# Four-quadrant 64x64 products in the delta stage of a diffusion trunk: two of four heads cross the partition halves

## The chip, the core and the metric

The kernel runs on one core of one Trainium2 chip. The metric is the device time of one execution in microseconds (us). Three runs of the kernel before gave 3064.36 us as median, from 3062.11 to 3075.93.

## The reference

Two layers of a transformer trunk over 512 latent and 256 context tokens of width 1024. Each layer projects its normalised input, feeds three token mixers (grouped-query attention, neighbourhood attention, and a bidirectional gated delta rule), merges their outputs, and ends with a squared-ReLU MLP. The change touches the delta rule alone. It works on chunks of 64 tokens, for 4 heads and in two directions. For each chunk and head it inverts a 64x64 triangular matrix by repeated squaring:

```
nil = where(strict, -einsum('bhid,bhjd->bhij', kb, kc) * decay, 0)
tinv = eye(CHUNK) + nil
power = nil
for _ in range(int(math.log2(CHUNK)) - 1):      # five times
    power = power @ power
    tinv = tinv + tinv @ power
w_v = tinv @ (vc * beta)
k_cd = tinv @ (kb * exp(gc))
```

The chunks' results then go through a recurrence over a 128x128 state per head.

## The kernel before, in words

Five engines run their own instruction streams and meet at semaphores. Nothing reorders them: the order of the work is the order in which the program is written for each engine. PE is the matrix engine (a weight load, PEld, goes with each matmul), DVE, ACT and POOL are the element-wise engines, SP issues the DMAs of the weights.

**Stages.** A layer runs: normalisation, the delta rule's projections and short convolution, the delta stage (this case), the attention projections, attention, gates and branches, output, MLP. Large products are done in three passes of split halves (L453 to L455).

**The delta stage.** A layer has 6 steps `s`. A step treats one tile of 128 tokens for each direction `d` (0 and 1), so the two partition halves (rows 0 to 63 and 64 to 127) hold two chunks, and 4 heads lie side by side: 8 matrices of 64x64 for each `d`. A step has a *powers phase* and a *recurrence*.

In the powers phase, iteration `i` (0 to 4) squares the power and its transpose and multiplies the inverse:
- PE, `halves` (L609): for each head and each half, one 64x64 product whose operands lie in one partition half and whose result lands in the same half. The array thus uses two of its four 64x64 quadrants. For each `d`: 8 products for the power, and 8 for its transpose (not in the last iteration), into one PSUM pair ("pw"); then, once these are read out, 8 products power x inverse into another ("X"). In the trace every float32 product leaves two records.
- ACT (L1266) copies the new power out of PSUM, DVE (L1686) the new transpose; DVE (L1690) adds the product to the inverse.
- In layer 0, in 20 of the 30 iterations (3 or 4 in each step, none in `i` = 4), PE also does a block of the later layers' modulation from weights that SP streams in (L490, `modulation`, 32 products of 32 columns on four column strips, 4 slots of 512 KB through a ring of 6), and later one transpose (L500).

PSUM is a ring of four pairs (`take`): each product group takes the next and waits until the group four before it was read. Before the powers phase, PE turns the matrix (L609 `ps<-cst,R`, "AT"), ACT copies it (L1252), DVE adds the identity (L1669). After it, PE computes k_cd (L798), then the recurrence: L817, L825, L837, L848, L859, with the next step's L633 (key products), read out by DVE (L1710, L1719 or L1721, L1649, L1658) and ACT (L1280). In layer 1 only the last four steps have outputs (L837, L859, L1719, L1721).

Of the kernel before, what the change touches and what calls it, by code (L numbers as in the profile page):

```python
# [21 lines left out]
P = 128  # L22
# [86 lines left out]
def program(nc, a, out, x_store, skew, bias_rows, z_store, book):  # L109
    book["final"] = book.get("final", False)  # L110
    with ExitStack() as ctx:
# [138 lines left out]
        def power(d, i):  # L250

            one, two = (pbuf[d], tbuf[d]), (p2buf[d], t2buf[d])
            return (*one, *two) if i % 2 == 0 else (*two, *one)

# [185 lines left out]
        def _(pe):  # L440
# [171 lines left out]

            def head_spread(l, j):
# [67 lines left out]
            for l in range(DEPTH):  # L681
# [83 lines left out]
                for s in range(TT):  # L765
                    turned = None
                    for i in range(5):
                        for d in range(2):
                            src, srcT, dst, dstT = power(d, i)
                            pe.wait_ge(*(read("pw", l, s, d, i - 1) if i else read("AT", l, s)))  # L770
                            ps = take(pe, "pw", l, s, d, i)
                            last = halves(ps, srcT, src)
                            if i < 4:
                                last = halves(ps[:, 512:768], src, srcT)
                            last.then_inc(*filled("pw", l, s, d, i))
                        for d in range(2):
# [14 lines left out]
                    for d in range(2):  # L791
                        pe.wait_ge(*pool_done.at("kbe", l, s, d))
                        pe.wait_ge(*read("X", l, s, d, 4))
# [259 lines left out]
        def _(act):  # L1053
# [88 lines left out]
            for l in range(DEPTH):  # L1142
# [105 lines left out]
                def delta_turned(l, s):  # L1248

                    act.wait_ge(*full("AT", l, s))  # L1250
                    for d in range(2):
                        A(flat(tbuf[d]), pair("AT", l, s)[:, 512 * d:512 * d + 256], ACT.Copy)\  # L1252
                            .then_inc(*free("AT", l, s, by=1))
# [157 lines left out]
        def _(dve):  # L1411
# [128 lines left out]
            for l in range(DEPTH):  # L1540
# [101 lines left out]
                def delta_decays(l, s, d):  # L1642

                    dve.wait_ge(*full("bc", l, s, d))
                    if s:
                        dve.wait_ge(*(pool_done.at("QW", l, s - 1, d) if want_out(l, tiles[0][s - 1]) else dve_done.at("A", l, s - 1, d)))
# [17 lines left out]
                def delta_turned(l, s, d):  # L1664
# [472 lines left out]
```

## Time and profile before

| | |
|---|---|
| median of 3 runs | 3064.36 us |
| span of the profiled execution | 3063.6 us |
| its own time beyond the span | not recorded; the median is 0.8 us above the span |
| PE busy | 2885.9 us (94%) |
| PEld busy | 2477.4 us (81%) |
| DVE, ACT, POOL busy | 1198.7, 1040.4, 1039.7 us (39, 34, 34%) |

A page has the busy times of each engine, the span in 40 slices, the DMA queues, the chain of work that ended last, and groups of instructions by line with their count, busy time and mean duration, and what ended the engine's idle time before them. The starts of instructions are read from a timeline. A matmul's duration holds its way through the array, so a busy PE may still be starting instructions more slowly than it could.

### The profile page before, as it was taken

How to read it: one execution, taken by the hardware profiler on the slowest of the kernel's cores; microseconds unless marked ns; L12 is line 12 of the kernel's file. 1: busy time of each engine (PE TensorE's matmuls, PEld its weight loads, DVE VectorE, ACT ScalarE, POOL GpSimd, SP SyncE). 2: the span in 40 equal slices, each digit the busy share in tenths (PEclk: the TensorE clock that was granted, in tenths of full speed). 3: DMA queues.
4: the chain of work that ended last, by engine and by line, in shares of the span. 5: the costliest groups of instructions: out<-in, count | busy, mean ns of one | idle time of the engine just before them, and what ended most of it. 6: DMA issues, size and time to landing. Idle time of an engine off the chain costs nothing. (4 is left out here: it accounts for less than half of the span.)

```text
span 3063.6 us, 57689 instructions
## 1 busy us (share of the span) xinstructions
PE 2885.9 (94%) x24931; PEld 2477.4 (81%) x24931; DVE 1198.7 (39%) x1821; ACT 1040.4 (34%) x1771; POOL 1039.7 (34%) x701
## 2 busy tenths in 40 slices
PE   6999888998899999999999999898999999999999
PEld 5877777886688888799999978788787788778887
DVE  4753443245631113422222268555245721242223
ACT  4542222225542112422222245433225532342223
POOL 3234434230313333222232322355330344434443
PEclk8999999999999999999999999999999999999999
DMA  6225434110012232122222122100220034323332
GB/s 251 62 87 197 141 138 125 49 49 1 12 36 62 62 106 67 49 65 67 62 69 62 62 90 62 37 3 10 83 56 8 13 98 139 93 82 97 96 99 81
DMA packets 303693, 231.96 MB, mean 76 GB/s; under 512 B 16785, under 2 KB 275281, under 8 KB 302545
## 3 DMA queue, kind: packets, MB, share of 16 engines
q1 hardware_dynamic: 296816, 203.53, 22.0%
q0 software_dynamic: 3776, 17.91, 1.6%
q10 hardware_dynamic: 2848, 6.82, 0.6%
q8 instruction: 199, 3.26, 0.4%
q14 instruction: 54, 0.43, 0.0%
HBM read 217.22 MB, written 11.98 MB: 75 GB/s over the span
## 5 line engine op out<-in xcount | busy, mean ns | idle before, releaser
L1892 POOL TENSOR_TENSOR wl<-wring,wh 128x1024 fp32r<-128x1024 f32 (+1 forms) x312 | 725.9, 2328 | 1342.3 <-ACT wh L1124 1335.8
L453 PE MATMUL ps<-hh,wh 128*128 128x496 f32 (+2 forms) x2344 | 832.2, 355 | 6.5 <-DVE R L1743 3.5
L455 PE MATMUL ps<-hh,wl 128*128 128x496 f32 (+2 forms) x2344 | 820.3, 350 | 0.0
L454 PE MATMUL ps<-hl,wh 128*128 128x496 f32 (+2 forms) x2344 | 820.2, 350 | 0.0
L453 PEld LDWEIGHTS ps<-hh,wh 128*128 128x128 f32 x2344 | 441.7, 188 | 69.6 <-issue 6.6
L454 PEld LDWEIGHTS ps<-hl,wh 128*128 128x128 f32 x2344 | 442.1, 189 | 57.1 <-issue 3.8
L455 PEld LDWEIGHTS ps<-hh,wl 128*128 128x128 f32 x2344 | 441.6, 188 | 54.1
L1124 ACT ACTIVATE wh<-wring 128x1024 fp32r<-128x1024 f32 (+1 forms) x312 | 307.7, 987 | 494.6 <-PE ps L455 455.1
L1813 DVE SCALAR_TENSOR_TENSOR R<-ps,modcs,R 128x512 f32<-128x512 f32 x216 | 136.3, 659 | 358.4 <-PE ps L455 335.9
L455 PE MATMUL ps<-fh,wl 128*128 128x496 f32 (+2 forms) x768 | 270.8, 353 | 0.0
L453 PE MATMUL ps<-fh,wh 128*128 128x496 f32 (+2 forms) x768 | 270.8, 353 | 0.0
L454 PE MATMUL ps<-fl,wh 128*128 128x496 f32 (+2 forms) x768 | 270.8, 353 | 0.0
L609 PE MATMUL ps<-R 64*64 64x64 f32 x5376 | 184.3, 223 | 26.8 <-issue 8.2
L609 PEld LDWEIGHTS ps<-R 64*64 64x64 f32 x5376 | 170.4, 138 | 42.8 <-issue 22.2
L1832 DVE TENSOR_TENSOR R<-R 128x768 f32<-128x768 f32 (+1 forms) x64 | 66.1, 1032 | 339.8 <-ACT R L1381 339.8
L1797 DVE TENSOR_TENSOR R<-ps,R 128x768 f32<-128x768 f32 (+1 forms) x48 | 39.6, 825 | 392.7 <-PE ps L455 392.7
L455 PEld LDWEIGHTS ps<-fh,wl 128*128 128x128 f32 x768 | 144.3, 188 | 18.3
L454 PEld LDWEIGHTS ps<-fl,wh 128*128 128x128 f32 x768 | 144.3, 188 | 18.2
L453 PEld LDWEIGHTS ps<-fh,wh 128*128 128x128 f32 x768 | 144.3, 188 | 18.2
L981 ACT ACTIVATE R<-ps,stat 128x768 f32<-128x768 f32 (+2 forms) x160 | 116.3, 729 | 116.8 <-DVE stat L1485 113.2
L1485 DVE TENSOR_REDUCE stat<-ps 128x1 f32<-128x768 f32 (+2 forms) x160 | 114.6, 741 | 33.5 <-PE ps L563 31.3
L1381 ACT ACTIVATE R<-ps 128x768 f32<-128x768 f32 (+1 forms) x64 | 44.9, 702 | 234.6 <-PE ps L455 171.8
(257 smaller groups left out, 3911.4 us busy)
## 6 DMA issues: line engine op xcount, KB each, us to landing
wring<-in_w_ffn SPq DMA_DIRECT2D x128, 512.0 KB, 3.8
wring<-in_w_in SPq DMA_DIRECT2D x116, 512.0 KB, 3.6
wboth<-in_w_mod SPq DMA_DIRECT2D x80, 512.0 KB, 6.5
wring<-in_w_branch SPq DMA_DIRECT2D x48, 256.0 KB, 2.6
wring<-in_w_out SPq DMA_DIRECT2D x16, 512.0 KB, 3.4
x_store<-R POOLq DMA_DIRECT2D x2, 3072.0 KB, 8.9
R<-x_store POOLq DMA_DIRECT2D x2, 3072.0 KB, 11.0
R<-in_w_mod ACTq DMA_DIRECT2D x7, 512.0 KB, 15.7
```

The costliest lines, as they stand in the source:

```text
L453: mm(ps[:, t0:t1], ahk, rh[:, k, t0:t1], start=(k == 0), stop=False)
L454: mm(ps[:, t0:t1], ahk, rl[:, k, t0:t1], start=False, stop=False)
L455: last = mm(ps[:, t0:t1], alk, rh[:, k, t0:t1], start=False, stop=(k == kn - 1))
L609: last = mm(out[lo:lo + HALF, h * HALF:h * HALF + HALF], left[lo:lo + HALF, h, :], right[lo:lo + HALF, h, :], start=True, stop=True)
L981: nc.scalar.activation(prob[br][p % 2][:, u, 0:n], score_ps(l, p)[u][:, 0:n], ACT.Exp, bias=stat[:, sl, 0:1], accum_out=stat[:, sl, 1:2])\
L1124: A(slot_view(wh, n % NSPL, *slot), w, ACT.Copy).then_inc(*act_done.mark("whi", *slot))
L1381: A(f, landed(nt, "ff1", l, j), ACT.Relu).then_inc(*free("ff1", l, j))
L1485: V.tensor_reduce(stat[:, sl, 0:1], ps[:, 0:n], AX.X, ALU.max, negate=True)\
L1797: V.tensor_tensor(g if n else acc, landed(nt, "br", l, x), g, ALU.mult).then_inc(*free("br", l, x))
L1813: V.scalar_tensor_tensor(out=xT[:, j, t0:t1], in0=landed(nt, *key)[:, t0:t1], scalar=modc[:, gate + j, c:c + 1], in1=xT[:, j, t0:t1], op0= ...
L1832: V.tensor_tensor(f, f, f, ALU.mult).then_inc(*dve_done.mark("fsq", l, j))
L1892: G.tensor_tensor(slot_view(wl, n % NSPL, l, name, i), w, slot_view(wh, n % NSPL, l, name, i).bitcast(F32), ALU.subtract)\
```

## The change

Heads 0 and 1 keep their products inside a half. Heads 2 and 3 are multiplied across: operands in the one half, result in the other, so that a group of four successive products names four different quadrants of the array (`quarters`). A product across moves a head's matrices to the other half, so the inverse can't be added to its product in place: for heads 2 and 3 the left factor is power plus identity (kept in `wbuf`, made by DVE from PSUM), and ACT copies the product out as the new inverse. The straight heads are still added by DVE. After an even number of crossings everything is back in its half; for that the first inverse of heads 2 and 3 comes from 8 more products in "AT".

The order moves too: PE now does the powers of iteration `i` for both directions and then the inverse's product of iteration `i - 1`, both directions in one PSUM pair. ACT and DVE wait for each other's copies only through PE. POOL forms `aqbuf * wbuf` of both directions ahead of its other query work, since `wbuf` is written in the powers now.

```diff
+            def quarters(ps, at, left, across, right):
+                for h in range(2):
+                    for lo in (0, HALF):
+                        up, c0 = HALF - lo, at + h * HALF
+                        mm(ps[lo:lo + HALF, c0:c0 + HALF], left[lo:lo + HALF, h, :], right[lo:lo + HALF, h, :],
+                           start=True, stop=True)
+                        last = mm(ps[up:up + HALF, 512 + c0:512 + c0 + HALF], across[lo:lo + HALF, 2 + h, :],
+                                  right[lo:lo + HALF, 2 + h, :], start=True, stop=True)
+                return last
...
                 for d in range(2):
                     pe.wait_ge(*dve_done.at("A", l, s, d))
-                    last = halves(ps[:, 512 * d:512 * d + 256], pbuf[d], over_heads(ident_half))
+                    halves(ps[:, 256 * d:256 * d + 256], pbuf[d], over_heads(ident_half))
+                    for h in range(2):
+                        for lo in (0, HALF):
+                            up, c0 = HALF - lo, 512 + P * d + HALF * h
+                            last = mm(ps[up:up + HALF, c0:c0 + HALF], pbuf[d][lo:lo + HALF, 2 + h, :],
+                                      ident_half[lo:lo + HALF, :], start=True, stop=True)
...
-                    for i in range(5):
-                        for d in range(2):
+                    for i in range(6):
+                        for d in range(2 if i < 5 else 0):
                             src, srcT, dst, dstT = power(d, i)
-                            pe.wait_ge(*(read("pw", l, s, d, i - 1) if i else read("AT", l, s)))
+                            if i:
+                                pe.wait_ge(*act_done.at("pw", l, s, d, i - 1))
+                                pe.wait_ge(*dve_done.at("pw", l, s, d, i - 1))
+                            else:
+                                pe.wait_ge(*read_first("AT", l, s))
                             ps = take(pe, "pw", l, s, d, i)
-                            last = halves(ps, srcT, src)
+                            last = quarters(ps, 0, srcT, srcT, src)
                             if i < 4:
-                                last = halves(ps[:, 512:768], src, srcT)
+                                last = quarters(ps, P, src, src, srcT)
                             last.then_inc(*filled("pw", l, s, d, i))
-                        for d in range(2):
-                            src, srcT, dst, dstT = power(d, i)
-                            pe.wait_ge(*read("pw", l, s, d, i))
-                            pe.wait_ge(*(read("X", l, s, d, i - 1) if i else dve_done.at("X0", l, s, d)))
-                            halves(take(pe, "X", l, s, d, i), dst, xbuf[d]).then_inc(*filled("X", l, s, d, i))
-                        if l == 0:
+                        if i:
+                            ps = take(pe, "X", l, s, i - 1)
+                            pe.wait_ge(*(read("X", l, s, i - 2) if i > 1 else read("AT", l, s)))
+                            for d in range(2):
+                                pe.wait_ge(*read("pw", l, s, d, i - 1))
+                                last = quarters(ps, P * d, power(d, i - 1)[2], wbuf[d], xbuf[d])
+                            last.then_inc(*filled("X", l, s, i - 1))
+                        if l == 0 and i < 5:
...
-                            A(flat(power(d, i)[2]), pair("pw", l, s, d, i)[:, 0:256], ACT.Copy)\
-                                .then_inc(*free("pw", l, s, d, i, by=1 if i < 4 else 2))
+                            n = 2 if i < 4 else 1
+                            A(squares(d, i, 0)[:, 0:n, :], pair("pw", l, s, d, i)[:, 0:P * n].rearrange("p (k n) -> p k n", k=n),
+                              ACT.Copy).then_inc(*act_done.mark("pw", l, s, d, i))
+                        if i:
+                            act.wait_ge(*full("X", l, s, i - 1))
+                            A(both(XB, 1), by_head(pair("X", l, s, i - 1)[:, 512:768]), ACT.Copy)\
+                                .then_inc(*free("X", l, s, i - 1, by=1))
...
-                    for d in range(2):
-                        delta_turned(l, s, d)
-                    for i in range(5):
-                        for d in range(2):
-                            if i < 4:
-                                dve.wait_ge(*full("pw", l, s, d, i))
-                                V.tensor_copy(flat(power(d, i)[3]), pair("pw", l, s, d, i)[:, 512:768])\
-                                    .then_inc(*free("pw", l, s, d, i, by=1))
-                        for d in range(2):
-                            dve.wait_ge(*full("X", l, s, d, i))
-                            V.tensor_tensor(flat(xbuf[d]), pair("X", l, s, d, i)[:, 0:256], flat(xbuf[d]), ALU.add)\
-                                .then_inc(*free("X", l, s, d, i))
+                    delta_turned(l, s)
+                    for i in range(6):
+                        for d in range(2 if i < 4 else 0):
+                            dve.wait_ge(*full("pw", l, s, d, i))
+                            V.tensor_copy(squares(d, i, 1), pair("pw", l, s, d, i)[:, 512:768].rearrange("p (k n) -> p k n", k=2))\
+                                .then_inc(*dve_done.mark("pw", l, s, d, i))
+                        if i:
+                            dve.wait_ge(*full("X", l, s, i - 1))
+                            V.tensor_tensor(both(XB, 0), by_head(pair("X", l, s, i - 1)[:, 0:256]), both(XB, 0), ALU.add)\
+                                .then_inc(*free("X", l, s, i - 1, by=1))
+                        for d in range(2 if i < 5 else 0):
+                            dve.wait_ge(*act_done.at("pw", l, s, d, i))
+                            if i == 0 and want_out(l, tiles[0][s]):
+                                dve.wait_ge(*pool_done.at("QW", l, s, d))
+                            V.tensor_tensor(wbuf[d][:, 2:4, :],
+                                            pair("pw", l, s, d, i)[:, 512:640].rearrange("p (h n) -> p h n", h=2), ident_heads,
+                                            ALU.add).then_inc(*free("pw", l, s, d, i))
```

The order of PE around a modulation block in a step of layer 0, before (`ps2` and the like are the PSUM pairs of the ring; L609 x16 is power and transpose of one direction, x8 the inverse's product of one; L500 and L490 are the modulation's):

```order
L490 MATMUL ps1<-wboth,ccol 32x128 x32
L609 MATMUL ps2<-R 64x64 x16
L609 MATMUL ps3<-R 64x64 x16
L609 MATMUL ps0<-R 64x64 x8
L609 MATMUL ps1<-R 64x64 x8
L500 MATMUL ps2<-cst,mrow 128x128
```

Now, at the like place (L508 and L518 are the former L490 and L500; L636 is a straight product, L638 one across):

```order
L638 MATMUL ps2<-R 64x64
L518 MATMUL ps3<-cst,mrow 128x128
L508 MATMUL ps0<-wboth,ccol 32x128 x32
L636 MATMUL ps1<-R 64x64
L638 MATMUL ps1<-R 64x64
L636 MATMUL ps1<-R 64x64
L638 MATMUL ps1<-R 64x64
```

The inverse's products of both directions (ps2) now stand as one group behind the powers, and straight and crossing products alternate; an iteration with a modulation block takes five pairs of the ring of four, so the block's pair is the one that held the powers of direction 0.

DVE in a powers phase of layer 0, before, from the identity's addition (L1669) to the second modulation evacuation:

```order
L1669 TENSOR_TENSOR R<-R,cst 128x256 x2
L1686 COPY R<-ps 128x256 x2
L1690 TENSOR_TENSOR R<-ps,R 128x256 x2
L1514 COPY mrow<-ps 128x128
L1686 COPY R<-ps 128x256 x2
L1690 TENSOR_TENSOR R<-ps,R 128x256 x2
L1518 TENSOR_TENSOR modcs<-ps,pcols 128x8
```

And now (L1714 and L1716 make the first inverse, L1730 are the copies, L1734 the inverse's addition, L1740 power plus identity, L1559 and L1563 the former L1514 and L1518):

```order
L1714 TENSOR_TENSOR R<-ps,cst 128x2x128
L1716 TENSOR_TENSOR R<-R,cst 128x2x128
L1730 COPY R<-ps 128x2x128 x2
L1740 TENSOR_TENSOR R<-ps,cst 128x128 x2
L1559 COPY mrow<-ps 128x128
L1730 COPY R<-ps 128x2x128 x2
L1734 TENSOR_TENSOR R<-ps,R 128x2x128
L1740 TENSOR_TENSOR R<-ps,cst 128x128 x2
L1563 TENSOR_TENSOR modcs<-ps,pcols 128x8
```

An iteration of DVE has two copies of 256 columns, one addition of 256 and two of 128, where it had two copies and two additions of 256.

## Rows read from the trace of the kernel before

**Rows 1.** The page's costliest groups (busy us, mean ns, idle before), the powers' products.
```profile
L609 PE MATMUL ps<-R 64*64 64x64 f32 x5376 | 184.3, 223 | 26.8 <-issue 8.2
```

**Rows 2.** Busy time by stretch, delta stages of layers 0 and 1: engines, PEclk, DMA share, GB/s.
```profile
222.00:484.00 262.00, 228.93 (x5515) 202.17 (x5516) 110.77 (x243) 61.33 (x146) 102.45 (x112) 0.96 0.49 170
1952.00:2145.00 193.00, 171.87 (x4202) 156.82 (x4204) 99.61 (x200) 65.95 (x149) 99.63 (x106) 0.99 0.02 6
```

**Rows 3.** Timeline, layer 1, second step: start us, us, engine, line, count, [idle before <-releaser].
```profile
1984.48 1.15 PE L609 MATMUL ps<-cst,R 64*64 64x64 f32 x32
1986.36 1.73 DVE L1669 TENSOR_TENSOR R<-R,cst 128x256 f32<-128x256 f32 x2 [0.47 <-ACT R L1252]
1986.39 14.67 PE L609 MATMUL ps<-R 64*64 64x64 f32 x448 [0.76 <-ACT R L1252]
...
1987.58 0.38 ACT L1266 ACTIVATE R<-ps 128x256 f32<-128x256 f32 x1 [1.25 <-PE ps L609]
1988.02 0.92 DVE L1686 COPY R<-ps 128x256 f32<-128x256 f32 x2
...
1990.66 0.42 DVE L1686 COPY R<-ps 128x256 f32<-128x256 f32 x1 [0.44 <-PE ps L609]
...
1993.73 0.42 DVE L1686 COPY R<-ps 128x256 f32<-128x256 f32 x1 [0.44 <-PE ps L609]
```

**Rows 4.** Groups by line and form (busy us, mean ns): other tiled products, a small PSUM copy.
```profile
L490 PE MATMUL ps<-wboth,ccol 128*32 128x128 f32 x1280 | 42.6, 280 | 6.2 <-issue 5.4 <-DMA wboth<-in_w_mod 0.7
L798 PE MATMUL ps<-R 64*128 64x64 f32 x384 | 26.3, 287 | 1.7 <-issue 1.6
L633 PE MATMUL ps<-R 128*64 128x64 f32 x704 | 25.9, 229 | 12.8 <-DVE R L1658 9.6 <-ACT R L1233 2.4
L1514 DVE COPY mrow<-ps 128x128 f32<-128x128 f32 x24 | 7.0, 292 | 47.3 <-issue 26.5 <-PE ps L490 20.8
```

**Rows 5.** Timeline of PE, 238.15 to 238.24 us: the head of a modulation block.
```profile
238.16 0.32 PE L490 MATMUL ps<-wboth,ccol 128*32 128x128 f32 x4
```

**Rows 6.** Timeline, layer 1, a step with outputs (2082 to 2099 us).
```profile
2082.53 1.41 DVE L1721 COPY R<-ps 64x512 f32<-64x512 f32 x2 [0.67 <-PE ps L859]
2083.37 2.08 PE L609 MATMUL ps<-R 64*64 64x64 f32 x64 [0.88 <-DVE R L1721]
...
2098.51 0.74 PE L798 MATMUL ps<-R 64*128 64x64 f32 x9 [0.18 <-issue]
```

**Rows 7.** Timeline of PE, layer 0: second, third and fourth step.
```profile
274.72 2.08 PE L609 MATMUL ps<-R 64*64 64x64 f32 x64 [0.88 <-DVE R L1721]
...
298.45 2.41 PE L798 MATMUL ps<-R 64*128 64x64 f32 x32
...
317.28 2.08 PE L609 MATMUL ps<-R 64*64 64x64 f32 x64 [0.88 <-DVE R L1719]
...
337.20 0.65 PE L490 MATMUL ps<-wboth,ccol 128*32 128x128 f32 x8 [2.26 <-issue]
...
345.91 2.00 PE L798 MATMUL ps<-R 64*128 64x64 f32 x32 [0.18 <-issue]
...
364.34 2.08 PE L609 MATMUL ps<-R 64*64 64x64 f32 x64 [0.88 <-DVE R L1721]
...
367.85 1.95 PE L490 MATMUL ps<-wboth,ccol 128*32 128x128 f32 x64
...
390.35 2.36 PE L609 MATMUL ps<-R 64*64 64x64 f32 x47 [2.07 <-issue]
...
393.05 1.33 PE L798 MATMUL ps<-R 64*128 64x64 f32 x10
```

**Rows 8.** DMA rate, 284 to 288 us in 40 slices; landing of all 80 modulation loads.
```profile
GB/s 430 410 389 410 430 410 389 410 410 410 410 410 410 410 410 410 389 328 451 144 102 82 82 21 41 20 20 20 41 20 20 20 41 20 20 0 0 0 0 0
DMA to landing us min/median/max: 3.6/6.5/13.4
```

**Rows 9.** Busy time by stretch, just after the idle time of 2.26 us in layer 0.
```profile
336.00:343.00 7.00, 5.80 (x104) 5.40 (x104) 1.56 (x4) 0.77 (x2) 0.00 (x0) 0.52 0.81 285
```

More of the change, by code:

```diff
@@ L253, in power, with squares, both, by_head @@
             return (*one, *two) if i % 2 == 0 else (*two, *one)
+        def squares(d, i, b):
+            at = U0 + 5120 * d + (3328 if i % 2 == 0 else 3072)
+            return R[:, at:at + 1024].rearrange("p (k n) -> p k n", k=2)[:, :, P * b:P * b + P]
+        def both(at, b):
+            v = R[:, U0:U0 + 10240].rearrange("p (d n) -> p d n", d=2)
+            return v[:, :, at + P * b:at + P * b + P].rearrange("p d (h n) -> p d h n", h=2)
+        def by_head(ps):
+            return ps.rearrange("p (d h n) -> p d h n", d=2, h=2)
+        ident_heads = ident_half.unsqueeze(1).to_broadcast([P, 2, HALF])
+        ident_both = ident_half.unsqueeze(1).unsqueeze(1).to_broadcast([P, 2, 2, HALF])
+        XB, TB = 4096, 3584
         ps_full = [ctx.enter_context(nc.semaphore(f"ps_full{i}")) for i in range(4)]
@@ L792, in _ @@
                         pe.wait_ge(*pool_done.at("kbe", l, s, d))
-                        pe.wait_ge(*read("X", l, s, d, 4))
+                        pe.wait_ge(*read("X", l, s, 4))
                         ps = take(pe, "kcd", l, s, d)
@@ L1251, in delta_turned @@
                     for d in range(2):
-                        A(flat(tbuf[d]), pair("AT", l, s)[:, 512 * d:512 * d + 256], ACT.Copy)\
-                            .then_inc(*free("AT", l, s, by=1))
+                        ins = A(flat(tbuf[d]), pair("AT", l, s)[:, 256 * d:256 * d + 256], ACT.Copy)
+                    ins.then_inc(*free("AT", l, s, by=1))
                 for d in range(2):
@@ L1662, in delta_keys, with delta_turned @@
                     V.tensor_tensor(pbuf[d], pbuf[d], p2buf[d], ALU.mult).then_inc(*dve_done.mark("A", l, s, d))
-                def delta_turned(l, s, d):
-                    dve.wait_ge(*read("AT", l, s))
+                def delta_turned(l, s):
+                    dve.wait_ge(*full("AT", l, s))
                     if s:
                         dve.wait_ge(*full("vn", l, 2 * s - 1))
-                    V.tensor_tensor(xbuf[d], tbuf[d], over_heads(ident_half), ALU.add)\
-                        .then_inc(*dve_done.mark("X0", l, s, d))
+                    V.tensor_tensor(both(XB, 1), by_head(pair("AT", l, s)[:, 512:768]), ident_both, ALU.add)
+                    dve.wait_ge(*read_first("AT", l, s))
+                    V.tensor_tensor(both(XB, 0), both(TB, 0), ident_both, ALU.add).then_inc(*free("AT", l, s, by=1))
                 for d in range(2):
@@ L1944, in delta_betas, with delta_queries, delta_queries_masked @@
                     if s:
-                        pool.wait_ge(*full("X", l, s - 1, d, 4))
+                        pool.wait_ge(*full("X", l, s - 1, 4))
                     G.tensor_tensor(p2buf[d], over_heads(masks[m_strict[d]]), along(nbeta[:, t, 4 * d:4 * d + 4], HALF),
                                     ALU.mult).then_inc(*pool_done.mark("MB", l, s, d))
-                def delta_queries(l, s, d):
-                    t = tiles[d][s]
-                    pool.wait_ge(*read("bc", l, s, d))
-                    G.tensor_tensor(qdbuf[s % 2][d], qT[:, :, t * P:t * P + P].rearrange("p h (c n) -> p c h n", c=2),
-                                    qdbuf[s % 2][d], ALU.mult).then_inc(*pool_done.mark("qd", l, s, d))
-                    pool.wait_ge(*read("Q", l, s))
-                    pool.wait_ge(*act_done.at("W", l, s, d))
-                    G.tensor_tensor(aqbuf[d], aqbuf[d], wbuf[d], ALU.mult).then_inc(*pool_done.mark("QW", l, s, d))
+                def delta_queries(l, s):
+                    pool.wait_ge(*read("Q", l, s))
+                    for d in range(2):
+                        pool.wait_ge(*act_done.at("W", l, s, d))
+                        G.tensor_tensor(aqbuf[d], aqbuf[d], wbuf[d], ALU.mult).then_inc(*pool_done.mark("QW", l, s, d))
+                    for d in range(2):
+                        t = tiles[d][s]
+                        pool.wait_ge(*read("bc", l, s, d))
+                        G.tensor_tensor(qdbuf[s % 2][d], qT[:, :, t * P:t * P + P].rearrange("p h (c n) -> p c h n", c=2),
+                                        qdbuf[s % 2][d], ALU.mult).then_inc(*pool_done.mark("qd", l, s, d))
+                def delta_queries_masked(l, s, d):
                     pool.wait_ge(*pool_done.at("QW", l, s, d))
```

11 lines of the change are left out of this document (6 added, 5 removed).

## The prediction, written before the changed kernel ran

> **What bounds the kernel now.** I read the groups by line first, then busy time by stretch, then the timeline of two powers phases. The products of the powers hold PE for 184.3 us, 34 ns a record [rows 1]; the two delta stages take 262 and 193 us, with PE busy 87 and 89% of them [rows 2]. In layer 1 a phase is one unbroken PE group: 448 records in 14.67 us, and two equal DVE copies of successive iterations start at 1990.66 and 1993.73, so an iteration (96 records) takes 3.07 us, 32 ns a record [rows 3]. DVE does 4 operations of 0.42 us in it and ACT 2 of 0.38, so PE sets the pace there, and what PE saves is saved until the next engine is late.
>
> **Can four quadrants run at once?** A 64x64 record starts every 29 ns: 32 of them take 1.15 us, less 0.22 for the last one's way through the array, over 32 [rows 1, 3]. The nearest rows for tiles are these. L633 has two column strips that read all rows: 25.9 us over 704, 37 ns with the waits' share. L798 has two row strips with weights of 128 columns: 68 ns. L490 has four column strips and moves 128 columns: 33 ns a record, against 280 ns for one [rows 4]; a block of 64 takes 1.95 us [rows 7], or 26.5 ns each ((1.95 - 0.28) / 63). Since twice the columns take less time a record on four strips than half of them on two, a strip's time and not the start of instructions bounds both: 4 x 26.5 = 106 ns for 128 columns, 2 x 29 = 58 for 64. And four records start within 0.04 us (0.32 less 0.28) [rows 5]. So I take 58 ns for four records, 14.6 each. Bounds: 10 ns (0.04 over 4, only starts count) and 29 (nothing overlaps further). I choose 14.6, since strips of both kinds are seen to overlap, though never in both directions together.
>
> The Trainium skill ("TensorE: Matmul & The Clock Gate", Part 3, what overlaps and what doesn't) says that a weight load runs beside a matmul in flight only if their row groups differ. Each half would then serve its two quadrants in turn and the change would bring nothing; the sum would be the third rival's. By that rule L633, which shares all its rows between two strips, would take the 58 ns of a quadrant for each record; it shows 37 with its waits, so the trace speaks against the rule here.
>
> **An iteration in layer 1.** PE: 96 records x 14.6 = 1.40 us. DVE: two copies 0.50 apart, start to start (0.92 for both, so 0.50 + 0.42) [rows 3], the addition 0.50, two additions of 128 columns at 0.29 (as L1514 [rows 4]) + 0.07 = 0.36 each: 3 x 0.50 + 2 x 0.36 = 2.22 us. ACT: 3 x 0.38, hidden. So DVE is late next. The ring ties too: powers of direction 1 wait for the pair freed by the first L1740, then need 0.47 on PE and 0.21 to DVE, which falls beside DVE's remaining work. I take 2.22, against 3.07.
>
> **A phase in layer 1.** PE's first group 0.47 + 0.21 until DVE can copy, but DVE must finish the first inverse: L1669's two additions took 1.73 us [rows 3], of which one is now from PSUM and early; say 1.0 until the first copy. Then i = 0: 2 x 0.50 + 2 x 0.36 = 1.72; three iterations 6.66; i = 4: PE's 0.47 (it waits for the last L1740), 0.21, 0.50, 0.72, with a signal's 0.06: 1.96; the last product 0.47 + 0.21 + 0.42 + 0.06 = 1.16. Sum 12.5 us, against 14.67 + 0.17 = 14.84: 2.3 less. "AT" has 16 records more, at 29 ns 0.47 us, and PE's next powers wait behind it: net 1.9. Three steps of this kind: 5.7. In the other three DVE is still busy with L1721 0.57 us into the phase (2082.53 + 1.41 = 2083.94 against 2083.37 [rows 6]), then has 0.42 and 0.55 to 1.0 of its own: first copy at 2.0, end at 13.5, against 2098.51 - 2083.37 = 15.14; net of AT 1.2 each, 3.6. Layer 1: 9.3 us.
>
> **A phase in layer 0.** Here modulation blocks (1.95 us) fill PE while DVE works, but their weights come by DMA. At 410 GB/s a slot of 0.52 MB takes 1.28 us once the queue runs, and 3.6 at least from issue to landing [rows 8]. The ring holds 6 slots, a block eats 4. From a block's start, slots 7 to 10 are asked for as its quarters are read, at 0.7 to 2.1 us; with 3.6 us for the first and a median of 6.5, I estimate that they land at 4.5, 7.1, 8.4 and 9.6, and the next each 1.25 later.
> - *Four blocks (two steps).* PE now reaches the first block after 0.93 + 0.1 instead of 3.51 us (364.34 to 367.85 [rows 7]). The second needs slot 8: ends at 7.5. The third needs slot 12, at 12.1: ends at 12.6. The fourth needs slot 16, at 17.1: ends at 17.6. DMA bounds it. Then powers and X of i = 4 0.94, DVE's work on them to 2.3, the last product 1.2: 3.5. Sum 1.0 + 17.6 + 3.5 = 22.1, AT 0.5, and 3.0 for the pauses of PE on "issue" with no releaser (2.07 [rows 7], and I allow 0.9 for shorter ones), which I leave: 25.6. Before: 393.05 - 364.34 = 28.7. Gain 3.1.
> - *Three blocks with a free iteration after the first (two steps).* Blocks end at 12.6; 1.0 + 12.6 + 3.5 + 0.5 + 1.3 for the pause = 18.9, against 298.45 - 274.72 = 23.7. Gain 4.8.
> - *Three blocks in a row, then a free iteration (two steps).* 1.0 + 12.6 + 2.2 + 3.5 + 0.5 + 2.4 = 22.2 against 345.91 - 317.28 = 28.6, of which 2.3 were a pause, and some 2.5 came from the clock of 0.52 behind it, at which PE's 5.8 busy us do the work of about 3.3 [rows 7, 9]. I keep the pause on both sides and the clock's loss too, since it came with the pause: 26.1 against 22.2. Gain 3.9.
>
> Twice each: 23.6 us. POOL's new order costs nothing: L1740 of i = 0 waits for its products, which end 2 us into the phase, before DVE comes to it. The recurrence is not touched.
>
> **Sum.** 9.3 + 23.6 = 32.9 us; 3063.6 - 32.9 = 3030.7 for the span, and 0.8 on top as the median of the runs has it: **3031.5 us**. Its own range, from DMA refilling 10% faster or slower and DVE's iteration between 2.0 and 2.6 us, is 3018 to 3045.
>
> **Rivals.**
> 1. *Instructions start no faster than they have been seen to for long, 26.5 ns a record.* For: no group in the rows is faster. Against: rows 5. An iteration is 2.54 us on PE, and with the waits behind it a layer 1 phase is about what it was, so AT makes it 0.5 worse: -3. In layer 0 DMA holds the blocks anyway; the first powers cost 0.8 and the tail 0.8 more than above: 6 x (3.9 - 1.6) = 14. Gain 11: **3053 us**. The Trainium skill ("TensorE: Matmul & The Clock Gate", Part 1) gives a floor of about 25 ns between starts of small matmuls; by it the gain would be some 15. That rows 5 has four starts in 40 ns says it isn't a floor for different tiles.
> 2. *More is won.* The pauses on "issue" fall into the DMA's waits, and DVE's iteration is 2.0: 6 x 2.5 + 6 x 1 more: **3010 us**.
> 3. *The quadrants don't overlap beyond two.* The same 448 records at 29 ns, with a longer tail (1.2) and AT (0.47), less 0.27 of waiting in each iteration: layer 1 +1.3 a step, layer 0 +0.2: +9, **3073 us**.
> 4. *Slower: the clock.* PE would idle 0.8 of 2.2 us in layer 1 and up to 2 us at a time in layer 0 for slots. After an idle 2.26 us the clock was granted at half for 7 us [rows 9]. If that comes in every phase and lasts through the recurrence (193/6 - 15 = 17 us a step [rows 2, 6], at half clock about +8), the 6 steps of layer 1 lose their gain and 48 us, and layer 0 keeps some 12: **3100 us**. It decides from the point where the clock is low in about four tenths of the stages (33 of 33 + 48). Against: the average clock over the stages is 0.96 and 0.99 [rows 2], pauses and all.
>
> **Chances.** Forecast 0.58, rival 1 0.15, rival 2 0.11, rival 3 0.10, rival 4 0.06. What a measurement can tell from no change is 0.5%, 15 us: below 3049 or above 3080. Faster: forecast and rival 2, and a quarter of rival 1, 0.73. Slower: rival 4 and the upper edge of rival 3, 0.08. Same 0.19. The range of 8 in 10 reaches over rival 1 and part of rival 2: 3013 to 3062.
>
> **What would show it.** Groups of 96 records of L636 and L638 in 1.4 us where nothing waits; DVE without idle time between L1730 and L1740 in layer 1, equal copies 2.2 us apart; in layer 0, PE idle before L508 with DMA as releaser, near 2 us after the second block's start. Wrong, if a record of the powers takes 25 ns or more, if PE's clock falls in the phases of layer 1, or if blocks in layer 0 follow each other faster than 5 us.

## The result, and the profile after

The changed kernel takes 3078.95 us (median of 20 runs), the kernel before 3064.71 us beside it: ratio 1.0040, 95% interval 1.0027 to 1.0053. The forecast was 3031.5, the range 3013 to 3062; it is slower, not faster. The profiled execution spans 3073.5 us against 3063.6. Of all runs below one is in a state by itself: the profiled one of e10_joint took 4704.06 us at a mean clock of 0.554, so its profile is not used, and one more run of that kernel (e13_joint_again) gives the profile.

The page after, TensorE's powers (the row of [rows 1] split over two lines, the other half of the records is on L638) and the two rows that the prediction did not use, the queue that brings instructions and the engine's count:

```profile
PE 2850.4 (93%) x25123; PEld 2432.9 (79%) x25123; DVE 1177.7 (38%) x1881; ACT 1061.4 (35%) x1831; POOL 1040.0 (34%) x701
q8 instruction: 200, 3.28, 0.4%
L636 PE MATMUL ps<-R 64*64 64x64 f32 x2688 | 110.8, 233 | 41.9 <-DVE R L1740 16.7
```

Busy PE fell, but PE now waits 41.9 us ahead of L636; of that DVE ends only 16.7. A record is a weight load and a matmul, so PE has 50,246 instructions for the 200 packets of 16.4 KB (3.28 MB): about 126 records a packet, if all of them are PE's (inferred from the count). Before has 199.

The two delta stages by stretch, as in [rows 2] (layers 0 and 1):

```profile
222.00:484.00 262.00, 205.06 (x5622) 177.18 (x5620) 99.30 (x273) 71.26 (x175) 101.97 (x112) 0.88 0.50 169
1952.00:2145.00 193.00, 150.19 (x4242) 132.52 (x4242) 91.53 (x235) 76.18 (x185) 95.30 (x106) 0.89 0.03 9
```

PE is busy 24 and 22 us less in the same stretch, the count of records hardly changed, and the granted clock fell from 0.96 and 0.99 to 0.88 and 0.89. The second step of layer 1 [rows 3] shows both causes. First its phase and its recurrence (from the phase's last product to the next phase), by stretch. Before:

```profile
1986.39:2001.24 14.85, 14.40 (x449) 13.61 (x449) 8.89 (x20) 3.84 (x10) 5.74 (x7) 1.00 0.01 3
2001.24:2016.54 15.30, 12.71 (x232) 10.98 (x232) 6.62 (x14) 6.68 (x15) 6.80 (x7) 1.00 0.01 2
```

After:

```profile
1996.10:2010.47 14.37, 8.50 (x448) 7.58 (x449) 7.84 (x24) 5.44 (x15) 5.50 (x7) 1.00 0.02 5
2010.47:2028.07 17.60, 15.86 (x248) 13.74 (x248) 6.59 (x14) 6.79 (x15) 5.44 (x6) 0.81 0.01 2
```

The same 448 records keep PE busy 8.50 us in place of 14.40: the four quadrants do overlap. But the phase is only 0.48 us shorter, and the recurrence after it, on which nothing was changed, takes 17.60 us at a clock of 0.81 in place of 15.30 at 1.00. Where PE waits inside that phase (timeline, rows with idle time before them; time, us, [idle <-releaser]):

```profile
1999.80 0.27 PE L636 MATMUL ps<-R 64*64 64x64 f32 x1 [1.14 <-issue]
2001.22 0.24 PE L636 MATMUL ps<-R 64*64 64x64 f32 x1 [0.37 <-DVE R L1740]
2003.96 0.27 PE L638 MATMUL ps<-R 64*64 64x64 f32 x1 [1.48 <-issue]
2006.38 0.24 PE L636 MATMUL ps<-R 64*64 64x64 f32 x1 [0.57 <-DVE R L1740]
2007.69 0.21 PE L638 MATMUL ps<-R 64*64 64x64 f32 x1 [0.79 <-issue]
2009.19 0.24 PE L636 MATMUL ps<-R 64*64 64x64 f32 x1 [0.82 <-DVE R L1740]
```

Three waits have no releaser, 3.41 us in all, and three end with VectorE, 1.76; the records between the ends of the first three number 126 and 125. The DMA view of the same phase has nothing but instruction packets (40 slices of 0.36 us):

```profile
DMA  0002000000000001000000000200000000000001
GB/s 0 0 0 46 0 0 0 0 0 0 0 0 0 0 0 46 0 0 0 0 0 0 0 0 0 46 0 0 0 0 0 0 0 0 0 0 0 0 0 46
q8 instruction: 4, 0.07, 1.8%
```

They come 3.6 to 5 us apart (slices 4, 16, 26, 40), and PE goes on some 2.5 us after each has begun. With 29 ns a record, as before, 126 records last 3.7 us and the next packet is there in time; with 14.6 ns they are used up in 1.8 us, and PE stands still. It is so in all twelve phases: PE has 26 waits of over 0.6 us without a releaser, 44.0 us in all, and each of them ends 2.2 to 2.7 us after an instruction packet has begun, a stretch that covers only about an eighth of the phases' time. Before has 8 of them, 11.8 us, and they end 2.2 to 2.5 us after a packet has begun.

Phases and recurrences summed over a layer's six steps (five recurrences), with the time at half clock over both, in us; and the waits of PE inside the twelve phases that are over 0.6 us and have no releaser:

| kernel | layer 0 phases, recurrences (half clock) | layer 1 phases, recurrences (half clock) | waits without releaser |
|---|---|---|---|
| before | 162.0, 96.4 (20.5) | 91.3, 86.0 (2.9) | 8, 11.8 us |
| after | 160.3, 97.7 (58.2) | 85.4, 93.2 (41.0) | 26, 44.0 |
| e1_straight | 172.6, 93.0 (20.5) | 97.3, 92.4 (25.4) | 10, 16.1 |
| e2_filler | 161.2, 94.7 (47.8) | 84.0, 85.6 (10.2) | 15, 30.8 |
| e13_joint_again | 154.1, 98.0 (43.5) | 75.6, 93.9 (33.9) | 18, 28.5 |
| e5_bf16_timed | 121.7, 98.6 (59.6) | 54.9, 98.0 (77.8) | 7, 6.9 |
| e6_bf16_filler | 121.3, 95.3 (47.8) | 58.6, 94.0 (35.8) | 4, 6.3 |
| e14_small | 186.7, 95.7 (71.7) | 110.8, 94.4 (78.6) | 26, 41.0 |
| e4_bf16 (e5's kernel) | 121.4, 100.6 (65.9) | 56.3, 99.2 (80.1) | 6, 7.4 |

Each row is one execution; the last one against e5's shows how far two executions of one kernel differ, 1.4 us or less in a layer's phases and 2.0 in its recurrences.

Of the 9.9 us between the two profiled spans, the stages' table holds 0.9; 3.1 more lie in the recurrence after layer 0's last phase (17.98 us to the next wide product, at half clock in part, where before has 14.88); and 6.5 in layer 0's MLP, where products of 496 columns start 224 ns apart on average in this execution and 220 in before's. The other stages give 0.6 back. The MLP's share is not the change's: two executions of one and the same kernel (e4 and e5 below) show it too,

```profile
L479 PE MATMUL ps<-fh,wh 128*128 128x496 f32 (+2 forms) x768 | 272.6, 355 | 0.0
```

in the first and

```profile
L479 PE MATMUL ps<-fh,wh 128*128 128x496 f32 (+2 forms) x768 | 270.8, 353 | 0.0
```

in the second.

### The profile page after: what moved, and what is told of

Read it like the earlier page. It is cut to its first block and busy times, and to the rows that moved or that the text cites. A ratio compares the mean times of both kernels' runs of the same rounds, so it can differ in the third digit from the quotient of the medians.

```text
span 3073.5 us, 58089 instructions
## 1 busy us (share of the span) xinstructions
PE 2850.4 (93%) x25123; PEld 2432.9 (79%) x25123; DVE 1177.7 (38%) x1881; ACT 1061.4 (35%) x1831; POOL 1040.0 (34%) x701
## 3 DMA queue, kind: packets, MB, share of 16 engines
q8 instruction: 200, 3.28, 0.4%
## 5 line engine op out<-in xcount | busy, mean ns | idle before, releaser
L636 PE MATMUL ps<-R 64*64 64x64 f32 x2688 | 110.8, 233 | 41.9 <-DVE R L1740 16.7
L636 PEld LDWEIGHTS ps<-R 64*64 64x64 f32 x2688 | 97.9, 145 | 56.3 <-issue 34.4
```

Of the source, the lines that this page charges most:

```text
L636: mm(ps[lo:lo + HALF, c0:c0 + HALF], left[lo:lo + HALF, h, :], right[lo:lo + HALF, h, :], start=True, stop=True)
```

## The experiments

The runs were made in four groups, each with its own runs of the kernel before beside it (medians 3060.0 to 3062.3 us, 3064.7 beside the changed kernel). So runs of different groups compare best by their ratios to before.

**The crossing undone.** The order, the operations and the count of instructions stay; two quadrants in place of four.

```
-  up, c0 = HALF - lo, at + h * HALF
+  up, c0 = lo, at + h * HALF            # and the same in AT
```

> The changed kernel with the crossing taken out (heads 2 and 3 stay in their half; order, waits, operations and instruction count as changed), so two quadrants work and a record takes 29 ns. Supply theory (PE's instructions come in blocks of 256, some 126 records, and a block can't be had faster than about every 3.8 us; the four quadrants drain a block in 1.9 us and PE pauses): at 29 ns a block lasts 3.7 us, so pauses of over 0.8 us inside the powers in layer 1 vanish or shrink under 0.3 us, the clock stays at full there, recurrences of layer 1 are back at 15.3 to 18.4 us, phases are 15 to 16 us, and the whole time is that of before plus 5 to 15 us. If the loss of the changed kernel came from the new order or the added operations alone (rival), this kernel is slower than the changed one by the 1 us or more per phase that the quadrants save, and its recurrences stay at 17.6 to 19.8 us.

Measured: 3082.09 us, ratio to before 1.0057 (1.0037 to 1.0077): 20 us above before by the medians and 17 by the ratio, more than the 5 to 15 expected. The phases are 12 us longer in each layer than with the crossing (table): that is what the quadrants give, 24 of the 41.5 us that lie between the forecast and its third rival. The waits without a releaser fall from 26 to 10, and none is left in layer 1, as expected. In the whole time little of it shows: by the ratios e1 is 5 us slower than the changed kernel, and the intervals overlap. Against the phases stand the recurrences, 5.5 us longer with the crossing, with 99.2 us at half clock in the table against 45.9 without it; and the profiled run of e1 is its slowest (3092.15 us). The rest of the change (order, added operations) costs in this run 10.6 us in layer 0's phases and 6.0 in layer 1's, and three of layer 1's recurrences fell to half clock in part though their phases are full of records. Why they did I can't say.

**The clock.** Idle products into PSUM columns nobody reads, ahead of the powers of i = 2 to 4.

```
+  if d == 0 and i > 1 and (l == 1 or (s, i - 1) not in mod_steps):
+      for _ in range(2):
+          mm(ps[:, 256:512], ident, cst[:, C_COS:C_COS + 256], start=True, stop=True)
```

> The changed kernel plus two wide products (128x128 by 256 columns, 0.85 us of the array, 8 instructions) ahead of the powers of iterations 2 to 4 wherever no modulation block stands there; their results are not used. Clock theory (the pauses lower the clock, and the lowered clock lengthens the recurrence behind): PE's idle time in the phases of layer 1 falls from some 5 us to 2, the clock is low for under 10 us of layer 1's delta stage instead of 41, recurrences there are 15.5 to 18.6 us, phases stay at 13 to 15, and the kernel is 8 to 15 us faster than the changed one, about as fast as before. If idle time inside the phases doesn't set the clock, it is as slow as the changed one or 5 us slower, with the same 41 us at half clock.

Measured: 3062.32 us, ratio 0.9995 (0.9979 to 1.0011), 14 us (by the ratios) to 17 (by the medians) below the changed kernel for 44 products more, 25.1 us of PE. The same step as above:

```profile
1983.79:1996.88 13.09, 11.35 (x461) 9.32 (x461) 7.87 (x24) 5.49 (x15) 5.40 (x7) 1.00 0.01 4
1996.88:2012.34 15.46, 12.78 (x249) 11.08 (x249) 6.69 (x14) 6.77 (x15) 5.40 (x6) 1.00 0.01 3
```

The recurrence is back at 15.46 us and a clock of 1.00. Against the changed kernel the recurrences of the table are 10.6 us shorter and the phases 0.5, though in layer 1 the waits without a releaser fall from 14.3 us to 1.5: there the idle products fill the time in which instructions come. So in layer 1 the clock took back more (7.2 us) than the phases had won (5.9).

**The supply of instructions by itself.** A kernel with nothing but streams of 320 products (640 records) each: two quadrants, four quadrants, and four with 128 and with 16 columns.

> Only streams of 320 products on PE, with no waits, each behind 24 wide products; nothing else of the kernel is computed. Supply theory: two quadrants with 64 columns 29 to 30 ns a record; four quadrants with 64 columns start at 14.6 for the first block and then average 28 to 33 ns, in bursts with a pause every 126 to 128 records; four with 128 columns 28 to 31; four with 16 columns no faster than four with 64, 28 to 33. If the array or the start of instructions is the limit and the supply is not, four quadrants with 64 columns hold 14.6 throughout, and 16 columns are faster still.

The rates came as expected, but for 27 ns with 128 and with 16 columns, where at least 28 was expected. Its timeline on PE (L32 the products; wide products stand between the streams), and the DMA busy share from 66 to 84 us in 40 slices of 0.45 us:

```profile
27.21 18.88 PE L32 MATMUL ps<-X 64*64 64x64 f32 x640
...
66.82 3.95 PE L32 MATMUL ps<-X 64*64 64x64 f32 x255
71.78 2.09 PE L32 MATMUL ps<-X 64*64 64x64 f32 x128 [1.01 <-issue]
75.79 2.09 PE L32 MATMUL ps<-X 64*64 64x64 f32 x128 [1.91 <-issue]
79.79 2.09 PE L32 MATMUL ps<-X 64*64 64x64 f32 x128 [1.91 <-issue]
...
104.46 17.70 PE L32 MATMUL ps<-X 64*64 64x128 f32 x640
...
142.88 2.52 PE L32 MATMUL ps<-X 64*64 64x16 f32 x159
146.64 2.05 PE L32 MATMUL ps<-X 64*64 64x16 f32 x128 [1.24 <-issue]
150.09 9.67 PE L32 MATMUL ps<-X 64*64 64x16 f32 x353 [1.40 <-issue]
```

```profile
DMA  0000000100000001000000001000000001000000
q8 instruction: 4, 0.07, 1.7%
```

Two quadrants: 29.2 ns a record without a pause. Four: 128 records in 2.09 us less the last one's 0.21, 14.7 ns each, then 1.91 us of nothing: one block in 4.00 us. With 128 columns the records start 27.3 ns apart and no pause shows. A quarter of the columns doesn't help: 3.45 us from 146.64 to 150.09 for 128 records, 27 ns. The last 353 records of this stream need a warning: from 148.7 us the clock is granted at half (0.50), and they start 26.7 ns apart without a pause, so they say nothing of the supply but that it keeps up with that. No engine, semaphore or data transfer is there to wait for, and the four packets of the DMA view begin 2.3 to 3.0 us before the four waits of the 64-column stream end; the cause is the count of instructions. Why a packet takes 4.00 us with 64 columns and 3.45 with 16 is not shown.

**A record priced in place.** Eight products of 4 columns added to each power of i = 0 to 3 of the changed kernel.

```
+  for h in range(C_H):
+      for lo in (0, HALF):
+          mm(ps[lo:lo + HALF, 256 + 4 * h:260 + 4 * h], srcT[lo:lo + HALF, h, :], src[lo:lo + HALF, h, 0:4], ...)
```

> The changed kernel with eight added products of 4 columns in each power of i = 0 to 3 (into PSUM columns nobody reads): 768 products, 1,536 records, next to no columns. Supply theory: each record costs 27 ns of supply, 41 us in all, less what falls where TensorE waits for other engines: 20 to 41 us slower than the changed kernel, 3100 to 3120. Strip theory (only columns and the loads of four tiles side by side count, 7 ns a record): at most 11 us, below 3092.

Measured: 3120.97 us, ratio 1.0187 (1.0166 to 1.0208); 42 us above the changed kernel by the medians, 45 by the ratios: 27 to 29 ns for each of the 1,536 records, with next to no columns. The strip theory at 7 ns is out. But this is no clean price of the supply. The waits without a releaser did not grow (41.0 us against 44.0), and the phases ran 100.1 us at half clock against 44.9. In the one phase of layer 1 that had the full clock throughout, the fifth, 128 more records cost 2.6 us (16.80 against 14.20), 20 ns each. And in e3 a record of 16 columns takes 14.5 ns even in a burst at full clock, so a theory of the array alone should have been priced at 22 us and not at 11. What decides between supply and array is e3 and the joint products below.

**Half the records.** The powers' and the inverse's factors read as bf16: one record a product in place of two, in lower precision. A single run of it (e4), then timed (e5).

```
+  wB, pB, p2B, tB, t2B, xB = (... .bitcast(bf16).rearrange("p (a b c) -> p a b c", a=4, c=2)[:, :, :, 1] ...)
-  src, srcT, dst, dstT = power(d, i)
+  src, srcT, dst, dstT = power_b(d, i)
```

> The changed kernel with the powers' and inverse's products in bf16 (upper halves of the float32 values), so each gives one record instead of two: half the instructions, and about a quarter of the array's work. Supply theory: a phase needs 248 records, two blocks, so pauses inside the phases vanish or are one a phase; phases in layer 1 are 11 to 12.5 us, set by DVE; in layer 0 the blocks of modulation are 5 us apart, set by DMA. The clock may be low more often, since the array does less. If the pauses are no matter of instruction supply, they stay as many and as long as in the changed kernel, three a phase and 1.0 to 1.7 us.

> The changed kernel with the factors of the powers and of the inverse read as bf16 (the upper halves of the fp32 words, so these products are of lower precision), timed. Supply theory (TensorE's instructions arrive no faster than about 27 to 29 ns for a load and its matmul, so halving the records frees the phases): 3015 to 3025 us, ratio to before 0.985 to 0.988, the single run before gave 3018. Rival (that run was an outlier, the phases were bound by VectorE and ScalarE all along): above 3040.

Measured: 3018.13 us, then 3011.75, ratio 0.9837 (0.9815 to 0.9858), 3 us below the range expected. The phases of layer 1 are 8.6 to 10.0 us where 11 to 12.5 were expected, and the waits without a releaser fall from 44.0 us to 6.9. The same step:

```profile
1944.73:1953.28 8.55, 4.71 (x224) 3.74 (x225) 7.21 (x24) 4.98 (x15) 5.50 (x7) 0.66 0.02 4
1953.28:1971.35 18.07, 16.27 (x248) 14.10 (x249) 6.59 (x14) 6.80 (x15) 5.44 (x6) 0.78 0.01 2
```

The phase takes 8.55 us even at a clock of 0.66: less than the 12.5 forecast for fp32. The recurrence pays 2.8 us for the clock. In layer 0 only now do the modulation weights bind: PE's idle time ahead of their products, by what ended it, after and then e5 (groups by line, 222 to 484 us):

```profile
L508 PE MATMUL ps<-wboth,ccol 128*32 128x128 f32 x1280 | 48.5, 302 | 26.6 <-issue 16.9 <-DVE R L1740 5.0 <-DMA wboth<-in_w_mod 3.3
```

```profile
L516 PE MATMUL ps<-wboth,ccol 128*32 128x128 f32 x1280 | 51.8, 305 | 25.6 <-DMA wboth<-in_w_mod 13.0 <-DVE R L1748 7.8 <-issue 2.8
```

**bf16 with idle products** ahead of the powers of i = 1 to 4.

> The same with two idle 128x128x256 products ahead of each power of i = 1 to 4 (where no modulation block stands), where TensorE waits for VectorE. Clock theory (what the bf16 version loses in the recurrences, +13 us over both layers against before, is the clock at half): the recurrences go back toward 86 and 95 us, the granted clock of the delta stages rises, and the time is 3000 to 3012. Rival (the fillers stand in the way: 24 to 28 times 0.85 us a layer where a phase has only some 0.8 us of TensorE's idle time an iteration, and each filler's own records draw on the same supply): 3020 to 3035.

Measured: 3002.63 us, ratio 0.9805 (0.9786 to 0.9825), the fastest of all, 9 us below e5: phase 9.69 us at a clock of 1.00, but the recurrence still at 0.81 in the step shown.

```profile
1946.93:1956.62 9.69, 7.54 (x240) 5.51 (x241) 7.29 (x24) 4.70 (x15) 5.40 (x7) 1.00 0.02 3
1956.62:1974.35 17.73, 15.86 (x249) 13.78 (x250) 6.68 (x14) 6.89 (x15) 5.43 (x6) 0.81 0.01 2
```

**bf16 without the crossing**, and **the kernel before with bf16**, in its own order.

> The same bf16 version with the two crossing heads put straight (two tiles of the array in place of four), order and instruction count unchanged. Supply theory: one iteration has 48 records, 1.3 to 1.4 us of supply, against 48 x 14 = 0.7 us of two tiles' strips, so the four tiles bring little: within 6 us of the crossing version (at most 0.1 to 0.2 us an iteration of the chain). Rival (what bounds is the strips' own time, as in fp32, where the crossing saved 12 us a layer): 12 to 24 us slower than the crossing version.

> The kernel before, its own order and straight products, with the factors of the powers and the inverse as bf16. If supply is what bounds both kernels, it gains as the changed one does, and the rest of the difference is the order: the order before reads powers, then multiplies the inverse (two stages in a row an iteration), so a phase is longer than the changed one's by the two reads it waits for: 3020 to 3035. Rival (the new order with power plus identity is worth nothing or costs, as the straight fp32 version's +17 us over before suggests): below the bf16 crossing version, 3000 to 3012.

Measured: 3015.17 us, ratio 0.9842 (0.9820 to 0.9865), and 3029.89, ratio 0.9893 (0.9873 to 0.9912). With half the records the crossing is worth 3.4 us or nothing, and the order is worth 15, where in fp32 it cost 20. Both as the supply theory had it.

**The control for the clock.** The idle products of e2 in the kernel before.

> Control: the kernel before with the same two idle 128x128x256 products ahead of the powers of i = 2 to 4 (where no modulation block stands) that made the changed kernel 17 us faster. Clock theory (they help by keeping the clock up where the changed kernel leaves TensorE idle; before has only 2.9 us at half clock in layer 1 and 20 us in layer 0): within -5 and +15 us of before (the fillers cost up to 0.85 us each time where TensorE has no idle time, 30 times; 25 us at most). Rival (they help for another reason that before shares, such as the placement of instructions): as much as 17 us faster.

Measured: 3083.27 us, ratio 1.0061 (1.0040 to 1.0083). Where the clock is already up they only cost: the phases of layer 1 are 114.6 us in place of 91.3. So nothing of the placement of instructions made e2 fast. The cost, 21 us (19 by the ratio), lies above the range expected.

**Fewer records in full precision.** For i = 1 to 3 the transposed power and the inverse's product of the two straight heads have the same weights, and become one product of 128 columns: 80 records an iteration in place of 96.

```
+  mm(ps[lo:lo + HALF, c0:c0 + 256].rearrange("p (k n) -> p k n", k=2)[:, :, 0:HALF], src[lo:lo + HALF, h, :],
+     R[lo:lo + HALF, a0:a0 + 2 * step].rearrange("p (k n) -> p k n", k=2)[:, :, 0:HALF], ...)
```

> The changed kernel at full precision with fewer instructions for the same arithmetic: in the powers of i = 1 to 3 the transposed power and the inverse's product of the two straight heads, which have the same stationary factor, become one product of 128 columns in place of two of 64; the iteration has 80 records in place of 96, VectorE reads the inverse's straight heads in two operations in place of one. Supply theory: 16 records at 27 to 29 ns less in 3 iterations of 12 steps, 0.45 x 36 = 16 us; less what VectorE's added operation takes: 3062 to 3072 us, phases of layer 1 down from 85 to 77 to 81 us. Rival (the pauses are caused by something else than the number of instructions, or VectorE paces the iteration): within 3 us of the changed kernel's 3079, or slower by VectorE's added operation.

> The kernel with the joint products once more, for its profile. Supply theory: the phases of layer 1 fall from the changed kernel's 85 us to 77 to 81 us and those of layer 0 by a few us, and the pauses without a releaser come less often in an iteration. Rival (its gain of 18 us on the changed kernel is the clock's): phases as before, less time at half clock in the recurrences.

Measured: 3061.28 us, ratio 0.9993 (0.9975 to 1.0011), 14 us (by the ratios) to 18 below the changed kernel; one more run, 3051.1 us, gives the profile. Its phases are 6.2 and 9.8 us shorter than the changed kernel's, the recurrences within 1 us (table). 576 records fewer at 27 to 29 ns are 16 us, and 16.0 came; the array's own time would hardly change, since two records of 64 columns (14.7 ns each) become one of 128 (27.3), and PE is busy 0.7 us less in the phases. The waits without a releaser fell by 15.5 us. The step:

```profile
1976.00:1987.45 11.45, 8.72 (x400) 7.93 (x401) 7.88 (x27) 5.25 (x15) 5.50 (x7) 1.00 0.02 5
```

**Both remedies.** Joint products with the idle products, in fp32 (i = 2 to 4) and in bf16 (i = 1 to 4).

> The same joint products and the idle products ahead of the powers of i = 2 to 4 (where no modulation block stands). If supply and clock are the two causes and they add: 3045 to 3055 us, faster than before by 0.3 to 0.5%. If the fillers eat what the fewer instructions free: 3058 to 3065, no faster than before.

> bf16 factors (lower precision), joint products and idle products ahead of the powers of i = 1 to 4. Against the bf16 version with idle products (3002.6): supply theory, 8 records of 27 to 29 ns less in 36 iterations, up to 8 us faster where supply still binds, 2995 to 3002; if with bf16 the chain of ScalarE and VectorE already paces the iteration, their added operation makes it 0 to 8 us slower.

Measured: fp32 3054.58 us, ratio 0.9965 (0.9949 to 0.9981), at the edge of the range for two causes that add, and faster than both kernels at full precision. By the ratios that is 23 us below the changed kernel, where the joint products alone gave 14 and the idle products alone 14: the two remedies add in good part. The rest the idle products take back in the phases (in one step 13.67 us with them and 11.45 without; in layer 1 83.6 against 75.6), while the recurrences of layer 1 win 4.9. bf16 3014.64, ratio 0.9833 (0.9803 to 0.9863): 12 us slower than e6 by the medians and 9 by the ratios, whose intervals overlap; phases of layer 0 are 127.0 us against 121.3. There PE waits for VectorE 19.3 us in place of 16.8 and for DMA 12.8 in place of 9.2; so the branch of the expectation that put 0 to 8 us on VectorE's added operation fits best, but that it is this operation is not shown.

## Why the prediction was wrong

*Can four quadrants run at once?* Right: 14.6 to 14.8 ns a record in bursts, in the kernel and alone. The Trainium skill's rule ("TensorE: Matmul & The Clock Gate", Part 3) that a weight load runs beside a matmul only in another row group would have given 29; the trace disagrees with it, 14.7 ns over 128 records. Its floor of about 25 ns between starts (Part 1) is not one either for different tiles; but the long-run rate of e3's four quadrants, 27 to 31 ns, lies near it.

*"So a strip's time and not the start of instructions bounds both"* is the step that failed. True of the array in a burst of 64 records, it was carried over to phases of 448. Rows 4, 5 and 7 held no stretch of more than 64 records faster than 29 ns, so they could not show what happens after the 126 that a packet holds. There the supply of instructions bounds: e3's four quadrants take 4.00 us for 128 records, 31 ns each, and the kernel's phases have 44.0 us of waits for it. Rival 1 had this mechanism, no faster than 26.5 ns a record for long; 27 to 31 was measured. It left layer 1's phases as they were (a loss of 3 with AT), and they gained 5.9; it gave layer 0 a gain of 14, and its phases gained 1.7. That rival 3's 3073 us lies nearest to the measured time is luck: it has the quadrants not overlapping.

*An iteration and a phase in layer 1.* VectorE at 2.22 us an iteration was to be late next. It is late (0.37, 0.57 and 0.82 us before the next powers), but the supply costs more (3.41 us in that phase): 12.64 to 14.89 us a phase where 12.5 and 13.5 were forecast. That the mechanism was right behind the supply bf16 shows: 8.6 to 10.0.

*A phase in layer 0.* The DMA of the modulation slots was to bound it. It released PE for 3.3 us of the 26.6 ahead of L508; 16.9 had no releaser. Forecast 135.4 us for the six phases (162.0 less the gain of 23.6 and the 3.0 for AT, which lies ahead of them), measured 160.3, with 29.7 us of waits for instructions in them; with half the records 121.7, and then DMA is the releaser most often (13.0). This is the largest part of the miss. *"The pauses of PE on issue, which I leave"* as a constant were this very supply, and grow as the records get faster: the two rows that could have warned, 2.26 and 2.07 us with no releaser [rows 7], were booked as fixed losses. Both end 2.3 us after an instruction packet has begun.

*The clock.* "The recurrence is not touched" is the second step that failed: the sum put nothing on it, and the recurrences took 7.2 us more in layer 1, 1.3 in layer 0's five and 3.1 in its last. Rival 4 had the mechanism and its place: PE idles in the phases, and the recurrence pays. It priced 48 us for layer 1 if every recurrence ran at half throughout; 28.4 us of layer 1's recurrences were at half clock, and cost 7.2. "Against: the average clock, pauses and all" was no argument, since the pauses before were few. Neither rival alone gives the result. The two together account for the profiled pair (7.6 us won in the phases, 11.6 lost in the recurrences), not for the whole of the measured loss.

*POOL's new order, ACT:* no wait on them in the phases shown. *What would show it wrong* named "if PE's clock falls in the phases of layer 1": it fell, 12.6 us of the phases and 28.4 of the recurrences. Not settled: the profiled pair puts about 3.4 us on the change (9.9 - 6.5), the ratio says 12; the rest is spread over executions (3060 to 3091 us) that have no trace. Also open is why e1's new order costs 17 us in fp32 phases, in which AT's added products are not counted.

## What to carry to other kernels

Count instructions as well as columns: when a stream of small products gets faster than 27 to 31 ns a record (load and matmul, as measured here) for longer than one instruction packet, expect a pause of a microsecond or more with no releaser. "issue" idle time that recurs every so many records is a rate limit and not a constant; look at the instruction queue's packets before anything is booked as hidden. And price what an engine's new idle time does to its clock in the work behind it.

## What the runs showed of the hardware that I had not expected

- Instructions come while the kernel runs, in packets of 16.4 KB, about 126 loads with their matmuls; a stream that needs more than one packet in 3.5 to 4.0 us pauses 1.0 to 1.9 us at each (e3), and every such wait ends 2.2 to 3.0 us after a packet has begun.
- Four 64x64 tiles run fully side by side: 14.7 ns a record against 29.2 for two, in fp32 with 64 columns, until a packet's records are used up.
- Added work made a kernel 14 to 17 us faster: 44 idle products, 25 us of TensorE's time. The clock stayed at 2.4 GHz through most recurrences of layer 1 (1.00 in the step shown), where it had fallen to 1.2 for part of each (0.81).
- Products of 496 columns start 220 or on average 224 ns apart for hundreds of us, in one execution or another of the same kernel: 6.5 us in layer 0's MLP here.
